# Output projection of a transformer block in three rounded passes instead of one full-precision product

## The reference, cut to what matters

```python
def mixer(h, w_in, w_out, lam, lam_init, subln_g, sinks):
    proj = jnp.einsum('bsd,de->bse', h, w_in)
    ...                                   # oa, ob, oc: 4 + 6 + 6 heads of 64 columns
    o = jnp.concatenate([oa.reshape(B, S, A_V_W), ob.reshape(B, S, B_W), oc.reshape(B, S, C_Q_W)], axis=-1)
    return jnp.einsum('bse,ed->bsd', o, w_out)

x = x + g1 * mixer(h, w_in[l], w_out[l], lam, lam_init, subln_g[l], sinks[l])
h = rmsnorm(x, norm2_g[l]) * (1.0 + sc2) + sh2
x = x + g2 * peer_ffn(h, peer_wq[l], peer_keys[l], peer_u[l], peer_v[l])
return rmsnorm(x, final_g)
```

## Time and profile before

| | |
|---|---|
| time, median of 3 runs | 1574.92 us (1574.33 to 1574.95) |
| the profiled execution's own time | 1574.18 us |
| its span | 1572.3 us |
| PE busy | 1534.1 us, 98% |
| DVE busy | 1324.6 us, 84% |
| ACT busy | 652.7 us, 42% |
| granted clock of PE | 0.998 of full speed |

### The profile page before, as it was taken

How to read it: one execution, slowest core, us unless ns; L and a number is a source line. 1 busy time by engine, 2 the same in 40 slices (tenths; PEclk the granted TensorE clock), 3 DMA queues, 4 the chain that set the end, 5 groups by cost and what they waited for, 6 DMA issues and landing times.

```text
span 1572.3 us, 24383 instructions
## 1 busy us (share of the span) xinstructions
PE 1534.1 (98%) x8195; PEld 1349.5 (86%) x8195; DVE 1324.6 (84%) x2859; ACT 652.7 (42%) x1135; POOL 485.9 (31%) x450
## 2 busy tenths in 40 slices
PE   4999999999999999999999999999999999999997
PEld 3888766688999999999999999999999998888886
DVE  6688645439999989899698888899999998999977
ACT  4444543233345666647433333334333432233232
POOL 1121300033451000020265545456666663233000
PEclk9999999999999999999999999999999999999999
DMA  9744420022355565667799999999999999999773
GB/s 366 279 165 144 148 95 27 0 82 87 108 173 172 197 229 196 232 225 272 269 399 341 336 348 343 346 342 367 372 375 374 365 349 352 377 350 354 242 241 105
DMA packets 160466, 398.76 MB, mean 254 GB/s; under 512 B 11753, under 2 KB 75369, under 8 KB 158705
## 3 DMA queue, kind: packets, MB, share of 16 engines
q1 hardware_dynamic: 112992, 227.06, 41.3%
q0 software_dynamic: 36864, 134.23, 23.0%
q10 hardware_dynamic: 10514, 36.30, 5.9%
HBM read 359.27 MB, written 38.27 MB: 253 GB/s over the span
## 4 chain that ended last, share of the span: by engine, by line
PE 82%; DVE 13%; DMA 2%; ACT 2%; issue 1%; ACTq 0%; DVEq 0%; SPq 0%
PE bank_S L871 16%; PE bank_T L871 11%; PE bank_O L822 6%; PE bank_O L820 6%; PE bank_O L821 6%; PE bank_T L849 6%; PE bank_G L871 5%; PE bank_S L820 3%; PE bank_S L821 3%; PE bank_S L822 3%; PE bank_O L617 2%; PE bank_S L584 2%; DVE mod_acc L1818 1%; DMA u_raw<-in_u_t 1%; DVE v_sb L1824 1%; DVE v_sb L1811 1%
## 5 line engine op out<-in xcount | busy, mean ns | idle before, releaser
L1407 ACT ACTIVATE v_hi<-v_raw 128x1024 fp32r<-128x1024 f32 x124 | 131.7, 1062 | 331.1 <-PE bank_G L871 331.0
L1379 ACT ACTIVATE u_hi<-u_raw 128x1024 fp32r<-128x1024 f32 x128 | 135.9, 1061 | 247.5 <-PE bank_O L822 115.5
L1175 POOL COPY stage<-eidx 128x1 uint32<-128x1 uint32 (+1 forms) x128 | 73.8, 576 | 465.4 <-DVE eidx L1939 209.0
L820 PE MATMUL bank_S<-h_hi,u_hi 128*128 128x384 f32 x512 | 180.2, 352 | 1.9 <-DVE u_lo L1911 1.9
L1179 POOL DMA_INDIRECT row<-in_peer_u,stage x128 | 148.2, 1158 | 103.7 <-POOL stage L1175 103.7
L822 PE MATMUL bank_O<-h_hi,u_lo 128*128 128x384 f32 x512 | 172.1, 336 | 0.0
L820 PE MATMUL bank_O<-h_hi,u_hi 128*128 128x384 f32 x512 | 172.0, 336 | 0.0
L822 PE MATMUL bank_S<-h_hi,u_lo 128*128 128x384 f32 x512 | 171.8, 336 | 0.0
L821 PE MATMUL bank_S<-h_lo,u_hi 128*128 128x384 f32 x512 | 171.8, 335 | 0.0
L821 PE MATMUL bank_O<-h_lo,u_hi 128*128 128x384 f32 x512 | 171.7, 335 | 0.0
L2007 DVE SCALAR_TENSOR_TENSOR y<-row,wgt,y 128x1024 f32<-128x1024 f32 x128 | 165.8, 1295 | 0.0
(11 more groups left out here) (333 smaller groups left out, 3588.6 us busy)
## 6 DMA issues: line engine op xcount, KB each, us to landing
u_raw<-in_u_t SPq DMA_DIRECT2D x128, 512.0 KB
v_raw<-in_peer_v SPq DMA_DIRECT2D x128, 512.0 KB
gates<-g_out ACTq DMA_DIRECT2D x12, 2048.0 KB, 6.8
g_in<-gates SPq DMA_DIRECT2D x32, 768.0 KB
ada_late<-in_w_ada SPq DMA_DIRECT2D x8, 2048.0 KB, 8.5
spill<-a_act ACTq DMA_DIRECT2D x56, 192.0 KB, 2.2
a_act<-spill SPq DMA_DIRECT2D x14, 768.0 KB, 10.1
w_raw<-in_w_in SPq DMA_DIRECT2D x20, 512.0 KB, 3.7
```

The lines of the kernel that those rows point to most:

```text
L820: pe.matmul(ps[:, 0:DT], u_hi[q][:, kk], h_hi[:, GT:NT, k, :], start=(k == 0), stop=False)
L1379: act.activation(u_hi[c % 2][:, :], u_raw[:, c % 2, :], ACT.Copy).then_inc(s_uhi, 1)
L1407: act.activation(v_hi_end[:, i % TAIL, :] if end else v_hi[:, c % 2, :], v_raw[c % 4][:, :], ACT.Copy)\
```

## The change

All 64 products of the output projection become three passes of f32r: o_hi·w_hi, o_lo·w_hi and o_hi·w_lo. For that:

- ACT rounds the eight tiles of `w_out` (`out_high`), at the end of its steps J = 34, 35, 39, 41, 42, 43, 44 and 45 (tiles 6, 7, 5, 0, 1, 2, 3, 4); DVE subtracts (`out_low`) one step later.
- ACT's copies of o now round it and no longer free the bank; DVE's new `o_low` reads the same bank behind them, writes the low part and frees it. It stands in the step behind ACT's copy (40, 49, 55, 61, 63, and for the last part between `norm_in` and `norm_out` of tile 2).
- The early products of tile 0 move from steps 40 and 42 to 41 and 43. The late columns of tile 0 are taken as (0 to 3) and (4).
- h2 of tiles 1 and 2 share a slot.
- `wq_hi[1]` now lies where `oT` is, so ACT waits for the last product of tile 2 before `wq_high(1)`. Tiles 2 and 3 of wq and `keys` are loaded when tile 3's last product is done.

```diff
-        oT = at("oT", 80, [P, KD, P])
+        oT = at("oT", 80, [P, KD, P], f32r)
+        oT_lo = [at(f"oT_lo{j}", kib, [P, KD // 2, P], f32r) for j, kib in enumerate((188, 198))]
...
-        wq_hi = [at(f"wq_hi{j}", kib, [P, D], f32r) for j, kib in enumerate((88, 80, 194))]
+        wq_hi = [at(f"wq_hi{j}", kib, [P, D], f32r) for j, kib in enumerate((88, 80))]
...
-        C_TILES, AB_TILES = (5, 6, 7), ((0, 1), (2, 3, 4))
+        C_TILES, AB_TILES = (5, 6, 7), ((0, 1, 2, 3), (4,))
+        OUT_AT = {34: 6, 35: 7, 39: 5, 41: 0, 42: 1, 43: 2, 44: 3, 45: 4}
+        H2_SLOT = [0, 1, 1, 3]
...
+            def out_passes(ps, hi, lo, k, half, start, stop):
+                at = slice(half * 512, half * 512 + 512)
+                pe.matmul(ps[:, :], hi, out_hi(k, half), start=start, stop=False)
+                pe.matmul(ps[:, :], lo, out_hi(k, half), start=False, stop=False)
+                return pe.matmul(ps[:, :], hi, wo_lo[k][:, at], start=False, stop=stop)
...
-                if since == -5:
+                if since == -4:
                     emptied(("oT_first", C_TILES[0]))
-                    pe.wait_ge(s_wout_c, 48)
+                    pe.wait_ge(s_wolo, 3)
                     out_proj_first(0, C_TILES, first=True)
-                if since == -3:
+                if since == -2:
                     out_proj_first(1, C_TILES, first=True)
...
                 if since == 4:
-                    pe.wait_ge(s_wout, 16 * 5)
+                    pe.wait_ge(s_wolo, 8)
...
-            for e in range(4):
+            for e in range(2):
                 sp.dma_start(wq_raw[:, e % 4, :], wq[e]).then_inc(s_wq[e % 4], 16)
-            for half in range(2):
-                taken(sp, ("oT", 1, half))
+            taken(sp, ("y", NT - 1, 1))
+            sp.dma_start(wq_raw[:, 2, :], wq[2]).then_inc(s_wq[2], 16)
             sp.dma_start(keys[:, :, :], keys_t).then_inc(s_keys, 16)
+            sp.dma_start(wq_raw[:, 3, :], wq[3]).then_inc(s_wq[3], 16)
...
-                                   ACT.Copy).then_inc(freeing(("oT", i, half)), 1)
+                                   ACT.Copy).then_inc(s_othi, 1)
...
+            def out_high(k):
+                if k > 4:
+                    act.wait_ge(s_wout_c, 16 * (3 if k == 5 else 2))
+                    act.wait_ge(s_accd, 12)
+                else:
+                    act.wait_ge(s_wout, 16 * 5)
+                    unit_done(act, 19)
+                if k == 4:
+                    taken(act, ("o", 2 * NT - 1))
+                raw = w_outs[k][:, :]
+                act.activation(out_hi(k), raw.rearrange("p (t c) -> p t c", t=NT) if k == 4 else raw, ACT.Copy)\
+                   .then_inc(s_wohi, 1)
...
                 if 0 <= J < N:
                     take_pT(J)
+                if J in OUT_AT:
+                    out_high(OUT_AT[J])
                 if J == TILE_END[0] - 6:
                     take_oT_first(C_TILES)
...
+            taken(act, ("y", NT - 2, 1))
             wq_high(1)
             take_oT_last(*LATE_O)
...
+            def out_low(k):
+                dve.wait_ge(s_wohi, OUT_ORDER.index(k) + 1)
+                raw, lo, hi = w_outs[k][:, :], wo_lo[k][:, :], out_hi(k)
...
+                dve.tensor_tensor(lo, raw, hi.bitcast(f32), ALU.subtract).then_inc(s_wolo, 1)
+            def o_low(key, hi, lo):
+                ps = taken(dve, key)
+                dve.wait_ge(s_othi, O_KEYS.index(key) + 1)
+                dve.tensor_tensor(lo, ps[:, 0:lo.shape[1] * P].rearrange("p (a b) -> p a b", b=P), hi.bitcast(f32),
+                                  ALU.subtract).then_inc(freeing(key), 1)
...
+                if J - 1 in OUT_AT:
+                    out_low(OUT_AT[J - 1])
+                if J - 1 == TILE_END[0] - 6:
+                    o_low(("oT_first", 5), oT[:, 5:8, :], oT_lo[1][:, 1:4, :])
+                if J - 1 == TILE_END[0] + 3:
+                    o_low(("oT_first", 0), oT[:, 0:4, :], oT_lo[0][:, :, :])
+                    o_low(("oT_first", 4), oT[:, 4:5, :], oT_lo[1][:, 0:1, :])
+                for i in range(1, NT - 1):
+                    if J - 1 == TILE_END[i] + 3:
+                        for half in range(2):
+                            o_low(("oT", i, half), oT[:, 4 * half:4 * half + 4, :], oT_lo[half][:, :, :])
+                if J == N - 1:
+                    for b, tiles in EARLY_O:
+                        o_low_last(b, tiles)
...
             norm_in(NT - 2)
+            o_low_last(*LATE_O)
             norm_out(NT - 2)
```

## The result

The changed kernel takes 1586.23 us (median of 6 runs, 1585.33 to 1587.62); before takes 1574.62 us (1573.39 to 1575.38). The ratio is 1.0075, 95% interval 1.0062 to 1.0088: slower by 11.6 us, where 7 were forecast, and 0.2 us above the forecast's range. The direction and the places were right; a cost was missing.

What follows compares the result with a forecast made beforehand. PE, busy 98% of the span, was taken as the bound. Terms -9.4 + 7.7 + 3.6 + 2.0 + 3.0 gave +6.9, about +7 us, so 1582 us (0.45% slower), range 1577 to 1586.

Steps and rivals of the forecast that it cites:

- 64 products in passes, at the full clock: Output projection: f32r passes 0.229 us apart save 10.9 us, slow group starts cost 1.5; net -9.4 us.
- waits in steps 39 to 49: PE waits for DVE's queue of splits and norms before tile 0's late columns: +7.7 us, 6.2 without the hold.
- step 55: PE's tile 1 products wait for two o_low behind tile 0's norm_out on DVE: +3.6 us.
- step 61: PE's tile 2 products wait for two o_low behind tile 1's norm_out on DVE: +2.0 us.
- tail: After tile 2's last product, wq tile 1's split delays add_mixer and the last group_out, so PE waits: +3.0 us.
- hold of 1.5 us: Steps 39 to 49: POOL's power holds DVE's out_low(0) until it ends, +1.5 us; the other end is 0.
- no idle time: DVE's list from PE's scores (44, 45) to group_out runs without gaps, 12.5 us before the hold.
- loads behind: wq and keys loads issued when query passes begin arrive in time: cost nothing; 6.5 us if landing one behind the other.
- DVE kept up: Rival: new subtractions fit DVE's idle time, so waits of steps 39 to 61 vanish: -6.4, 1568.5 us; 7%.
- Late loads: Rival: loads behind the output projection arrive late, +1 to +6.5 us more, centre 1586; 7%.
- passes not cheaper: Rival: new passes at 0.286 us save nothing, 1592.7 us; at 0.429 it is 27.5 more; 3%.
- signs of being wrong: DVE gaps in steps 42 to 48, PE's waits before 308 us under 9.4 us, or changed length behind query passes.

Runs made afterwards that it cites:

- e5: Changed kernel with norm_out of tiles 0 and 1 behind o_low, wq tile 1's split behind tile 2's h split, out_low(3) and (4) later: 1570.56 us, ratio 0.9974.
- e3: Changed kernel without the low parts of w_out tiles 0 to 4 (DVE subtracts 32 columns, third pass rereads the high part): 1579.58 us, ratio 1.0020.
- e6: Changed kernel with out_low(3) and out_low(4) moved to steps 47 and 49: 1583.28 us, ratio 1.0056.
- e4: Changed kernel with 14 and 8 unused PE passes put ahead of PE's two waits for o_low: 1579.82 us, ratio 1.0026.
- e2: Changed kernel with rounding and low part of wq tile 1 moved behind tile 2's h split: 1582.51 us, ratio 1.0036.
- e8: Changed kernel again, unaltered, on the second chip used for experiments: 1585.66 us, ratio 1.0057 to the kernel before.
- e7: Kernel before, with PE's products of tiles 1 and 2 waiting for h2 of the tile before: 1579.74 us, ratio 1.0025.
- e1: Changed kernel with norm_out of tiles 0 and 1 one step later, behind the next tile's two o_low: 1578.21 us, ratio 1.0018.

## Why the prediction was too small

By its own steps, against the changed kernel's profile:

| step | forecast | measured |
|---|---|---|
| 64 products in passes, at the full clock | -9.4 | -9.9 (from e5) |
| waits in steps 39 to 49 | +7.7 | +4.8 (0.51 + 0.68 + 0.67 + 1.88 + 1.27, less the 0.21 of before) |
| step 55 | +3.6 | +3.60 |
| step 61 | +2.0 | +1.94 |
| tail | +3.0 | +2.8 (2.12 + 0.66) |
| sum of these | +6.9 | +3.2 |
| work at the lower clock | no term | +8.6, the rest to 11.8 |

**The step that failed** is "Stationary tiles and widths are the same as in the new passes, so I take it over": the 0.229 us of a pass was taken from a stretch in which PE never waits, for passes that the same forecast put behind waits of 2 to 4 us. The clock of 1.00 in the earlier trace rows goes with 0.5 us of idle time and with none. The rest of 8.6 us can be had in a second way: half of the 17.9 us in which PE is busy at half clock would be 8.9. In e3 and e6 the same two ways give 5.1 and 5.0 us by difference, and 5.1 as half of 10.2 busy us at half clock. Of the 8.6 us, 5.0 are the 25 passes at 0.43 instead of 0.23 us. The other 3.6 I put down to scores, transposes, value products and the starts of groups in the same places, by difference: the scores at 231.48 are recorded with 1.23 us, where those at 226.69 have 0.70. e4 gives 4.1 us back by keeping the clock up in two of the three places.

**The window of steps 39 to 49** came out 6.6 us later, where 6.9 was forecast, but not by its terms, and that it came out near is luck. The forecast's hold of 1.5 us did not happen. DVE's timeline has the first of two splits, and the start of the second, beside POOL's power, which runs from 220.05 to 223.00:

```profile
220.05 2.95 POOL L1175 TENSOR_TENSOR sso<-sso,power 128x16 f32<-128x16 f32 x1 [30.93 <-DVE sso L1857]
...
221.65 2.36 DVE L1806 TENSOR_TENSOR wo_lo<-w_outs,wo_hi 128x1024 fp32r<-128x1024 f32 x2
```

2.36 us for two is their own time (one alone takes 1.22 us, and the next starts 1.13 behind it). The Trainium skill (SBUF — State Buffer, Who interferes with whom) would have the second engine blocked for the whole instruction; for a subtraction of 1024 columns the trace agreed, for a power on 16 columns it does not (the split runs its own 1.2 us while the power is recorded as running), and the measurement decides. PE's waits are 4.8 us where 7.7 were forecast, and the late columns are as late even so, because small products at half clock filled the place: 2.6 us by difference, and half of PE's 5.0 busy us at half clock up to there is 2.5. And e3 shows that the list was less of a bound than the sum of its durations made it: a list is dense only until something else in it waits. The forecast's "no idle time" held with the splits and not without them.

**Steps 55, 61 and the tail** were right to 0.2 us in size, and right in who ends the wait. They came from reading which instructions stand in DVE's order ahead of the one that frees PE's bank, with durations from rows. The loads behind cost nothing, as forecast: 1264.7 us from the query passes to the end, 1264.8 before.

**The rivals.** DVE kept up in none of the three places. *Late loads* and *passes not cheaper* did not occur. None of the rivals was the one that came: that an idle PE is a slower PE. Nor did one of the forecast's own signs of being wrong show (DVE's gaps, the sum of PE's waits, the length behind the query passes); none of them looked at the clock. The Trainium skill (TensorE: Matmul & The Clock Gate, Part 1) says that the array's default state is throttled and activity releases it, between two levels, 1.2 and 2.4 GHz. The clocks of 0.50 and 1.00 behind waits and behind work agree with it. It speaks against a change that adds waits, and the forecast had no term for it.

What stays open: why the series of slow passes are 7, 10 and 8 long and not others, and why behind the same waits the clock falls in one execution and not in another. The waits of 3.60 and 1.94 us have a fall beside or behind them in all five executions profiled with both (changed kernel, e2, e3, e6, e8), the tail's of 2.12 us in one of six (e6). And length alone doesn't tell: in the first place the clock fell behind waits of 0.69 and 0.65 us in e2 and of 0.40 and 0.97 us in e3, and stayed up behind three of 0.67 to 0.74 us in e5 and e6. That a kernel's spread comes from this was seen (e2, e8; and e5 without it lies within 1570.0 to 1571.2, but for one run of 1573.1) and not tried.

## What to carry to other kernels

A wait that a change adds to a PE-bound stretch can cost, beside its own length, the work behind it at half the clock: in this kernel a wait of 2 us cost up to 4. Several waits of 0.4 to 1 us close together brought it too, in some executions. So when PE's work is made cheaper by giving more to another engine, first list what that engine has in its order ahead of the instruction that frees PE, and move what is not urgent behind it; here three such moves turned 0.75% slower (0.57% on the chip of e5) into 0.26% faster, with the same instructions. And when the runs of one program fall into groups some us apart, look at their granted clocks. Where a wait can't be removed, work for PE that nobody uses may be worth putting into it.

## What the runs showed of the hardware that was not expected

- During or behind PE's idle times of 1.88, 3.60, 1.94 and (e7) 2.02 us the granted clock fell to half, and products behind started 0.43 instead of 0.23 us apart (f32r) and, in e7, four f32 products took 5.40 instead of 3.44 us. The fall can come in the middle of the work behind the wait, 1.2 us after it in e3.
- It also fell behind idle times of 0.69 and 0.65 us (e2) and of 0.40 and 0.97 us (e3), and did not behind three of 0.67 to 0.74 us (e5, e6), nor behind 1.14 and 0.42 us (e1, e5). After 2.12 us in the tail no pass was slow in the changed kernel, and six in e6.
- Fourteen and eight passes that nobody uses, in place of idle time, went with a clock of 1.00 behind them and 4.1 us less (e4).
- Runs of one program on one chip differed by 4 to 9 us with the mean granted clock: 0.996 and 0.997 in the two short runs of e8, 0.991 to 0.993 in the four long ones.
- A GpSimd power on 128x16, recorded for 2.95 us, did not hold a VectorE subtraction with two SBUF operands; a GpSimd subtraction of 128x1024 did.
